# Stream pieces in other slots and load order, routing in column groups with the bias rows behind the first gather, and other ScalarE and VectorE orders around attention

## The chip, the cores and the metric

One core of one Trainium2 chip runs the whole program in one launch. The metric is the device time of an execution in microseconds (us). A core has TensorE (PE, products; PEld is its weight load), VectorE (DVE), ScalarE (ACT), GpSimd (POOL, hardly used here) and SyncE (SP), which in this kernel issues every large DMA. Each engine works off its own queue in order and waits on semaphores.

## The reference

`first_block` and then `second_block` on 256 tokens of 1024 channels, all in fp32. Cut to what matters:

```python
# first block
proj = rmsnorm(x) @ w_mix_in            # short conv, gated delta rule, stick-breaking attention -> y
x = x + y @ w_mix_out
u = causal_dwconv(rmsnorm(x) @ w_ffn_up)
x = x + (silu(gate) * val) @ w_ffn_down
x = rmsnorm(x) * w_norm_final
# second block
sh1, sc1, gt1, sh2, sc2, gt2 = split(silu(c) @ w_ada + b_ada)
h = rms_norm(x, g_pre_mix) * (1 + sc1) + sh1
dq, dk, dv, nq, nk, nv = split(h @ w_in)      # differential and 2-D neighbourhood attention
mix = concat(o_diff, o_nat) @ w_out
x = x + gt1 * rms_norm(mix, g_post_mix)
h2 = rms_norm(x, g_pre_ffn) * (1 + sc2) + sh2
logits = h2 @ w_router + b_router             # 32 experts, top 4, softmax of the four
y[e] = swiglu_clamped(h2[tokens of e] @ w1[e] + b1[e]) @ w2[e] + b2[e]
x = x + gt2 * rms_norm(sum_k gate_k * y[expert_k], g_post_ffn)
```

## The kernel before

**Weights.** All weights ahead of the experts are 46 pieces of 2 MB (128 x 4096 fp32), and the parts are called `inp` (first projection, 7 pieces), `ada` (modulation, 12), `mo` (mix-out, 2), `up` (11), `dn` (down, 6), `in2` (second block's projection, 6) and `out` (2). The table `N_OF` gives each piece a number n. Piece n lies in slot n % 4 of a ring, and SP's `load(n)` (L317) first waits for `used(n - 4)`: the products that read the piece that lies there. The order in which SP loads is written out by hand (L322 to L376) and need not be that of the numbers. The experts' weights are 192 pieces of 2 MB in 10 slots (the four of the ring, four more, and slots 8 and 9 in the work area); a pass of the expert stage takes one expert's tokens in groups of 32 (53 passes here), and one expert has 6 pieces.

**Products.** Dense fp32 products are made of three: a weight piece is split into `w_hi` (ScalarE's copy, L1344, on VectorE for a few) and `w_lo` (VectorE, L1350), and the same is done to the activations (`x_hi`, `x_lo`). `rows_hi` and `rows_lo` (L1355, L1361) do it for mix-out and out. Two `w_hi` buffers take turns. `ada(j)` (L805) is a product of few rows. On TensorE `in2_hi(j, ..)` and `in2_lo(j, ..)` are the parts of projection piece j (L945, L946); its last part signals `proj2`, which both frees the slot and lets ScalarE copy the result (`projected(g)`, L1588, two for each piece).

**Attention.** TensorE weaves the projection and attention together in a fixed order: `score_pair(u)` (L988), `turn(v)` (transposes of probabilities, L1001), `diff_apply(v)` (L1013), `nat_apply`. Two waits of that order matter: `proj2_in` at 4 ahead of `score_pair(0)` and at 6 ahead of `diff_apply(0)`. ScalarE's order there:

```python
w_hi(a, i_in2 + 3)
projected(2)
projected(3)
probs(0)
probs(1)
w_hi(a, i_in2 + 4)
probs(2)
projected(4)
probs(3)
projected(5)
evac(0)
```

**Routing.** After `out`'s products and a norm come the logits (L1125), transposes of the activations (L1130), a mask of the top four on VectorE, positions of the tokens (L1135 to L1141), the sorting of the experts by load on VectorE, the table of passes (`cum`), the place of each token by pass (PP) and its gate (GP) (L1166 to L1170), the bias rows of b2 that open the four output banks (L1178), and then the first gather (L1185) with its transpose (L1192) and the first pass (L1210).

Of the kernel before, what the change touches and what calls it, by code (L numbers as in the profile page):

```python
# [26 lines left out]
P = 128  # L27
# [47 lines left out]
def first_block_and_moe(nc, consts, vecs, stream, bada, rows, natb, w1, w2, b1, b2, x, out):  # L75
    ctx = ExitStack()
    with ctx:
# [9 lines left out]
        def S(name):  # L87
            if name not in sems:
# [9 lines left out]
            pe_step=("ab ab_sum gcol gb kk krow xi_t vrow qsum at uw b0 a12 qq13 qq2 s2 o0 s3 o modc0 modc1 modc2 lams yd_turned lg pos posrow pmt cum pp"),  # L98
            act_step=("ab_in e_gates gl decays ksilu silc dt krow_in vsilu xi_in sk_root qsilu q_squares vrow_in "
                      "uw_in s1 s2_in s3_in o_squares o_root elam d_root yd_hi ee"),  # L100
            dve_step=("wab gu a8 egl dt_arg scales xit qs atm qe a1 qq13_in a2 qq2_in o_var sc_prod "
                      "lamp nlam d_var d_scaled yd_lo mask lgs cnr perm cum_in"))
# [25 lines left out]
        def three(ap, a):  # L128
            return ap.rearrange("p (a b) -> p a b", a=a)
# [100 lines left out]
        OUT_HI = (HI[0], LO[0])  # L230
# [11 lines left out]
        B1 = at(EX, 2048)  # L242
# [8 lines left out]
        LG, MASK, EE, GATE, PM = (three(temp(64), T) for _ in range(5))  # L251
# [15 lines left out]
        H2R = XN  # L267
        slot_base = [len([n for n in range(NSTREAM) if n % NSLOT1 == s]) if s < NSLOT1 else 0 for s in range(NSLOT)]
# [43 lines left out]
        def _(sp):  # L312
# [22 lines left out]
            for piece_ in (("dn", 0), ("dn", 1), ("dn", 2), ("dn", 3), ("in2", 0), ("dn", 4), ("dn", 5), ("ada", 8), ("ada", 9), ("ada", 10)):  # L335
                load(N_OF[piece_])
# [4 lines left out]
            for piece_ in (("out", 0), ("in2", 3), ("in2", 4), ("in2", 5), ("out", 1)):  # L341
                load(N_OF[piece_])
# [9 lines left out]
            expert_piece(0, 2)  # L352
            expert_piece(1, 7)
            sp.wait_ge(S("sc_in"), 16)
            for part in range(3):
                sp.dma_start(B1[NE * part:NE * part + NE, :], b1).then_inc(S("b1_in"), 16)
# [7 lines left out]
            expert_piece(0, 0)  # L364
# [3 lines left out]
            sp.dma_start(B2[0:NE, :], b2).then_inc(S("b_in"), 16)  # L368
# [181 lines left out]
        def _(pe):  # L550
# [303 lines left out]
            ada(2)  # L854
            pe.wait_ge(S("mo_gdn"), 2)
            mo_rows(0, 0)
            sb_tail(0)
# [68 lines left out]
            ada(9)  # L926
            ada(10)
            pe_norm(3)
            ada(11)
# [109 lines left out]
            in2_hi(0, 0, 4)  # L1039
            in2_lo(0, 0, 4)  # L1040
# [79 lines left out]
            hT_ready(pe, 4)  # L1120

            wr = three(vec("router"), KC)
            for t in range(T):
                for k in range(KC):
                    last = mm(flat[:, 2048 + 32 * t:2048 + 32 * t + 32], HT[:, k, 128 * t:128 * t + 128], wr[:, k, :],  # L1125
                              start=(k == 0), stop=(k == KC - 1))
            last.then_inc(*signal("lg"))
            for t in range(T):
                for k in range(KC):
                    last = nc.tensor.transpose(flat[:, 1024 * t + 128 * k:1024 * t + 128 * k + 128],  # L1130
                                               HT[:, k, 128 * t:128 * t + 128], ident)
                last.then_inc(S("h2r"), 1)
# [1256 lines left out]
```

## Time and profile before

| | |
|---|---|
| median of 3 runs | 1542.11 us (1541.65 to 1543.21) |
| the profiled execution's own time | 1541.02 us |
| its span | 1539.2 us |
| TensorE busy | 1337.1 us (87%) |
| VectorE busy | 542.9 us (35%) |
| ScalarE busy | 440.4 us (29%) |
| chain that ended last | PE 52%, DMA 36%, DVE 7%, ACT 3%, issue 2% |
| DMA | 509.28 MB, 331 GB/s over the span |

The profiled execution is 1.1 us below the median of the runs and 1.8 us above its span. Shares are averages over the program: the rows further down are taken by stage. The first block's mixer runs to about 196 us, up and down to 401, the second block's norm and modulation to 419, projection and attention with the out products to 552, routing to 594, the expert passes to 1526. PEclk in a row of windows is the granted clock of TensorE, as a share of 2.4 GHz (0.50 is 1.2 GHz).

### The profile page before, as it was taken

How to read it: one execution, taken by the hardware profiler on the slowest of the kernel's cores; microseconds unless marked ns; L12 is line 12 of the kernel's file. 1: busy time of each engine (PE TensorE's matmuls, PEld its weight loads, DVE VectorE, ACT ScalarE, POOL GpSimd, SP SyncE). 2: the span in 40 equal slices, each digit the busy share in tenths (PEclk: the TensorE clock that was granted, in tenths of full speed). 3: DMA queues.
4: the chain of work that ended last, by engine and by line, in shares of the span. 5: the costliest groups of instructions: out<-in, count | busy, mean ns of one | idle time of the engine just before them, and what ended most of it. 6: DMA issues, size and time to landing. Idle time of an engine off the chain costs nothing.

```text
span 1539.2 us, 30880 instructions
## 1 busy us (share of the span) xinstructions
PE 1337.1 (87%) x13128; PEld 779.5 (51%) x13128; DVE 542.9 (35%) x1075; ACT 440.4 (29%) x730; POOL 0.2 (0%) x4
## 2 busy tenths in 40 slices
PE   6999889999998868889988898789878798787985
PEld 5998569998688653334333333223323243232331
DVE  5842558784666752112121121112112121111212
ACT  5734334453355531112122111112111122121121
POOL 0000000000000000000000000000000000000000
PEclk9999999999999987899999999889999899999997
DMA  7322684454862476997999999999999999999996
GB/s 325 129 111 108 276 369 171 172 208 167 329 246 88 161 322 260 427 384 289 400 428 427 420 407 427 427 427 402 427 428 428 427 407 428 427 427 407 412 427 280
DMA packets 35988, 509.28 MB, mean 331 GB/s; under 512 B 4032, under 2 KB 4032, under 8 KB 4832
## 3 DMA queue, kind: packets, MB, share of 16 engines
q1 hardware_dynamic: 35904, 508.00, 79.5%
q8 instruction: 73, 1.20, 0.3%
q14 instruction: 11, 0.09, 0.0%
HBM read 506.93 MB, written 1.05 MB: 330 GB/s over the span
## 4 chain that ended last, share of the span: by engine, by line
PE 52%; DMA 36%; DVE 7%; ACT 3%; issue 2%; SPq 0%; DVEq 0%; ACTq 0%
DMA low<-in_w 26%; PE acc L1210 14%; PE acc L469 8%; PE acc L1227 7%; DMA high_part<-in_w 7%; DMA low<-in_stream 3%; PE acc L505 3%; PE acc L908 3%; PE acc L945 2%; PE acc L916 1%; PE acc L506 1%; PE acc L1200 1%; PE acc L832 1%; PE acc L805 1%; ACT w_hi L1344 1%
## 5 line engine op out<-in xcount | busy, mean ns | idle before, releaser
L1210 PE MATMUL acc<-low,high_part 128*32 128x512 f32 x2720 | 342.9, 636 | 74.6 <-DMA low<-in_w 64.6
L2238 DVE TENSOR_SCALAR high_part<-acc 128x256 f32<-128x256 f32 x53 | 22.5, 425 | 689.5 <-PE acc L1210 689.5
L1210 PEld LDWEIGHTS acc<-low,high_part 128*32 128x32 f32 x2720 | 93.0, 114 | 281.4 <-issue 194.8
L1227 PE MATMUL acc<-low,high_part 128*32 128x256 f32 x2752 | 165.4, 389 | 28.3 <-DMA low<-in_w 27.9
L1718 ACT ACTIVATE high_part<-high_part 128x256 f32<-128x256 f32 x53 | 22.1, 418 | 451.7 <-DVE high_part L2238 451.7
L1350 DVE TENSOR_TENSOR w_lo<-low,w_hi 128x4096 fp32r<-128x4096 f32 x30 | 132.6, 4424 | 36.8 <-ACT w_hi L1344 36.7
L1227 PEld LDWEIGHTS acc<-low,high_part 128*32 128x32 f32 x2752 | 84.2, 111 | 94.5 <-DMA low<-in_w 36.5
L1344 ACT ACTIVATE w_hi<-low 128x4096 fp32r<-128x4096 f32 x28 | 101.6, 3629 | 55.7 <-DMA low<-in_stream 33.0
L1210 PE MATMUL acc<-high_part 128*32 128x512 f32 x672 | 86.9, 641 | 18.4 <-DMA high_part<-in_w 16.4
L469 PE MATMUL acc<-x_hi,w_hi 128*128 128x256 f32 x352 | 86.8, 287 | 7.1 <-DVE x_lo L1378 7.1
L469 PE MATMUL acc<-x_lo,w_hi 128*128 128x256 f32 x352 | 86.6, 287 | 0.0
L1727 ACT ACTIVATE high_part<-acc 128x256 f32<-128x256 f32 x53 | 20.4, 386 | 210.2 <-PE acc L1227 210.2
L1200 PE MATMUL acc<-high_part 32*128 32x256 f32 x864 | 78.3, 432 | 0.6 <-ACT high_part L1727 0.5
L469 PEld LDWEIGHTS acc<-x_hi,w_hi 128*128 128x128 f32 x352 | 69.0, 196 | 8.0 <-DVE w_hi L1342 8.0
L469 PEld LDWEIGHTS acc<-x_lo,w_hi 128*128 128x128 f32 x352 | 69.0, 196 | 0.0
L1718 ACT ACT_TABLE_LOAD x53 | 68.0, 1283 | 1.4 <-issue 0.5
L1200 PEld LDWEIGHTS acc<-high_part 32*128 32x128 f32 x864 | 34.3, 186 | 59.4 <-issue 57.9
L1185 PE MATMUL acc<-high_part 128*32 128x256 f32 x864 | 59.4, 394 | 0.0
L1210 PEld LDWEIGHTS acc<-high_part 128*32 128x32 f32 x672 | 23.2, 114 | 69.5 <-issue 46.7
L505 PE MATMUL acc<-x_hi,w_hi 128*128 128x256 f32 x176 | 44.2, 290 | 0.0
L469 PE MATMUL acc<-x_hi,w_lo 128*128 128x256 f32 x352 | 44.0, 283 | 0.0
L1966 DVE SCALAR_TENSOR_TENSOR low<-acc,high_part,low 128x255 f32<-128x255 f32 (+1 forms) x88 | 36.4, 476 | 21.4 <-ACT low L1566 21.1
(454 smaller groups left out, 1766.2 us busy)
## 6 DMA issues: line engine op xcount, KB each, us to landing
low<-in_w SPq DMA_DIRECT2D x154, 2048.0 KB, 27.8
low<-in_stream SPq DMA_DIRECT2D x46, 2048.0 KB, 7.9
high_part<-in_w SPq DMA_DIRECT2D x38, 2048.0 KB, 29.8
high_part<-in_natb SPq DMA_DIRECT2D x1, 2048.0 KB, 17.6
high_part<-in_rows SPq DMA_DIRECT2D x1, 1536.0 KB, 18.4
high_part<-in_consts SPq DMA_DIRECT2D x1, 1060.0 KB, 6.9
high_part<-in_x SPq DMA_DIRECT2D x1, 1024.0 KB, 4.8
out<-high_part SPq DMA_DIRECT2D x2, 512.0 KB, 2.7
```

The costliest lines, as they stand in the source:

```text
L469: return nc.tensor.matmul(o, w[:, k, cols], x[:, k, :], **flags)
L505: return nc.tensor.matmul(o, w[:, k, cols], x[:, k, :], skip_group_check=True, **flags)
L908: last = mm(bank(2 * t + h), g[:, k, 128 * t:128 * t + 128], wh[:, o:o + 512], start=(k == 0 and g is gh), stop=False)
L945: return mm(o, w[:, k, cols], x[:, k, :], skip_group_check=True, **flags)
L1185: last = mm(flat[32 * q:32 * q + 32, 3072:3328], SEL[:, t, :], H2R[:, t, 256 * q:256 * q + 256], start=(t == 0), stop=(t == T - 1))
L1200: last = mm(flat[:, o:o + 256], SGT[r, 128 * t:128 * t + 128], YS[r, :], start=False, stop=False, skip_group_check=True)
L1210: last = mm(flat[32 * q:32 * q + 32, 2048:2560], XG[:, b, 32 * kk:32 * kk + 32], wp[:, 2048 * b + 512 * q:2048 * b + 512 * q + 512], start ...
L1227: last = mm(flat[32 * q:32 * q + 32, 3072:3328], AT[:, 128 * (c % 2) + 32 * (c // 2):128 * (c % 2) + 32 * (c // 2) + 32], wp[:, 1024 * (c ...
L1344: eng.activation(HI[i % 2], slot, ACT.Copy).then_inc(S("hi_act"), 1)
L1350: v.tensor_tensor(LO[s], ring[:, s, :], HI[i % 2].bitcast(F32), ALU.subtract).then_inc(S("lo_ready"), 1)
L1718: f(SIG, GLU, ACT.Sigmoid, scale=1.702).then_inc(S("sig"), 1)
L1966: last = stt(uc[:, 256 * c + sh:256 * c + 256], flat[:, o + 256 * c:o + 256 * c + 256 - sh], fc3[:, j, 3 * c + tap:3 * c + tap + 1], uc[:, ...
```

## The change

It renumbers the stream pieces (which slot each lies in and so which products its load waits for), reorders SP's loads, and reorders and reshapes work around them. The core of the diff:

```diff
-for _part, _ns in (("inp", range(PIN)), ("ada", (7, 9, 11, 13, 15, 12, 17, 19, 37, 34, 36, 41)), ("mo", (8, 10)),
-                   ("up", (14, 16, 21, 23, 18, 20, 25, 27, 22, 24, 29)), ("dn", (31, 26, 28, 33, 30, 32)),
-                   ("in2", (35, 40, 38, 39, 44, 42)), ("out", (45, 43))):
+for _part, _ns in (("inp", range(PIN)), ("ada", (7, 9, 11, 13, 15, 17, 19, 14, 37, 34, 32, 41)), ("mo", (8, 10)),
+                   ("up", (12, 21, 23, 18, 16, 25, 27, 22, 20, 29, 31)), ("dn", (26, 24, 33, 35, 30, 28)),
+                   ("in2", (39, 36, 38, 40, 42, 44)), ("out", (45, 43))):
...
-        OUT_HI = (HI[0], LO[0])
+        OUT_HI = (HI[0], LO[2])
...
-        B1 = at(EX, 2048)
+        B1 = W(6, 2048)
...
-            for piece_ in (("inp", 5), ("inp", 6), ("ada", 0), ("mo", 0), ("ada", 1), ("mo", 1), ("ada", 2), ("ada", 3), ("ada", 4),
-                           ("ada", 5), ("ada", 6), ("ada", 7)):
+            for piece_ in (("inp", 5), ("inp", 6), ("ada", 0), ("mo", 0), ("ada", 1), ("ada", 2), ("mo", 1), ("ada", 3), ("ada", 4),
+                           ("up", 0), ("ada", 5), ("ada", 6), ("ada", 7)):
                 load(N_OF[piece_])
-            sp.wait_ge(S("sb_y"), 2)
+            sp.dma_start(MODR[1], bada[:, 512:1024]).then_inc(S("bada_in"), 16)
             sp.dma_start(at(BC, 3072), rows).then_inc(S("rows_in"), 16)
-            load(N_OF["up", 0])
-            sp.dma_start(MODR[1], bada[:, 512:1024]).then_inc(S("bada_in"), 16)
...
-            for piece_ in (("out", 0), ("in2", 3), ("in2", 4), ("in2", 5), ("out", 1)):
+            for piece_ in (("out", 0), ("out", 1), ("in2", 3), ("in2", 4), ("in2", 5)):
                 load(N_OF[piece_])
...
-            sp.dma_start(B2[0:NE, :], b2).then_inc(S("b_in"), 16)
+            for q in range(4):
+                sp.dma_start(B2[NE * q:NE * q + NE, :], b2).then_inc(S("b_in"), 16)
...
-            ada(2)
             pe.wait_ge(S("mo_gdn"), 2)
             mo_rows(0, 0)
+            ada(2)
...
+            pe_norm(3)
             ada(10)
-            pe_norm(3)
-            ada(11)
...
             in2_hi(0, 0, 4)
+            ada(11)
             in2_lo(0, 0, 4)
...
-            hT_ready(pe, 4)
             wr = three(vec("router"), KC)
+            for b in range(4):
+                pe.wait_ge(S("hT_act" if b % 2 else "hT_dve"), 2 * 1 + b // 2 + 1)
+                for k in (2 * b, 2 * b + 1):
+                    q = k % 4
+                    last = mm(flat[32 * q:32 * q + 32, 2048:2304], wr[:, k, :], HT[:, k, :], start=(k < 4), stop=(k >= 4))
+            last.then_inc(*signal("lgp"))
...
             for t in range(T):
-                for k in range(KC):
-                    last = mm(flat[:, 2048 + 32 * t:2048 + 32 * t + 32], HT[:, k, 128 * t:128 * t + 128], wr[:, k, :],
-                              start=(k == 0), stop=(k == KC - 1))
+                last = mm(flat[:, 2560 + 32 * t:2560 + 32 * t + 32], LP[:, 128 * t:128 * t + 128], STACK, start=True, stop=True)
             last.then_inc(*signal("lg"))
...
-            pe.wait_ge(S("h2r_in"), 2)
-            pe.wait_ge(S("b_in"), 16)
-            pe.wait_ge(S("b1_parts"), B1PARTS)
-            for t in range(T):
-                for h in range(2):
-                    mm(bank(2 * t + h), GTT[0:32, 128 * t:128 * t + 128], B2[0:32, 512 * h:512 * h + 512],
-                       start=True, stop=False, skip_group_check=True)
...
             gather_transpose()
+            pe.wait_ge(S("b_in"), 64)
+            for q in range(4):
+                t, h = divmod(q, 2)
+                r = slice(32 * q, 32 * q + 32)
+                mm(bank(q), GTT[r, 128 * t:128 * t + 128], B2[r, 512 * h:512 * h + 512], start=True, stop=False, skip_group_check=True)\
+                  .then_inc(S("b2_in"), 1)
+            pe.wait_ge(S("b1_parts"), B1PARTS)
...
             evac(1)
+            w_hi(a, i_in2 + 5)
+            projected(6)
             probs(6)
             probs(7)
+            projected(7)
+            evac(2)
             diff_o(1)
-            w_hi(a, i_in2 + 5)
-            projected(6)
-            projected(7)
-
-            evac(2)
...
+            a.wait_ge(*step("pmt"))
+            f(PMT[0:32], flat[0:32, 3584:3840], ACT.Copy)
+            f(GTT, flat[:, 3840:4096], ACT.Copy).then_inc(*signal("pmt_in"))
...
-            rows_lo(N_OF["out", 0], OUT_HI[0], "out_w_hi0", 1, "out_w_lo0")
             softmax(8)
...
             weigh(11)
+            rows_lo(N_OF["out", 0], OUT_HI[0], "out_w_hi0", 1, "out_w_lo0")
             v.wait_ge(*step("yd_hi"))
...
-            v.wait_ge(*step("pmt"))
-            link(v.tensor_copy(PMT[0:32], flat[0:32, 3584:3840]))
-            v.tensor_copy(GTT[0:32], flat[0:32, 3840:4096]).then_inc(S("pmt_in"), 1)
```

Not shown: the residual after mix-out now has VectorE's `w_hi` of up(0) ahead of it; the split of b1 (VectorE) moves from behind attention to ahead of it and b1 is loaded behind down's pieces; `rows_lo` of out(1) moves behind `nat_lo(1)`; the gates are transposed four times over, so that each row group has its copy; the activations' transposes are split into three groups around the logits and positions; ScalarE copies H2R[0]; `select(0)` stands right behind the copy of PP; expert 0's piece 0 is loaded first among its pieces and piece 2 last but one, in place of the other way round.

Three places show how the work moves. The first is SP's queue around the end of the first block's mixer; L320 (L321 after) is `load`, and the words in brackets are the semaphores that it waits for. Before:

```order
L320 DMA low<-in_stream 128x4096 [waits proj] x6
L320 DMA low<-in_stream 128x4096 [waits ada] x3
L320 DMA low<-in_stream 128x4096 [waits mo_k]
L320 DMA low<-in_stream 128x4096 [waits ada] x2
L330 DMA high_part<-in_rows 128x3072 [waits sb_y]
L320 DMA low<-in_stream 128x4096 [waits mo_done]
L332 DMA low<-in_bada 128x512
```

After:

```order
L321 DMA low<-in_stream 128x4096 [waits proj] x5
L321 DMA low<-in_stream 128x4096 [waits ada]
L321 DMA low<-in_stream 128x4096 [waits proj]
L321 DMA low<-in_stream 128x4096 [waits ada] x2
L321 DMA low<-in_stream 128x4096 [waits mo_k]
L321 DMA low<-in_stream 128x4096 [waits ada] x2
L321 DMA low<-in_stream 128x4096 [waits mo_done]
L330 DMA low<-in_bada 128x512
L331 DMA high_part<-in_rows 128x3072
```

The load that waits for mo_k is ada(5) before and up(0) after; the one that waits for mo_done is up(0) before and ada(7) after. The transfer of `rows` has lost its wait and stands behind them.

The second place is ScalarE's queue at the start of attention; w_hi_50 and w_hi_49 are the two buffers of L1344 (L1355 after). Before:

```order
L1344 ACTIVATE w_hi_50<-low 128x4096 [waits lo_ready,hi_used,slot3_loaded]
L1588 ACTIVATE low<-acc 128x512 [waits proj2] x2
L1594 ACTIVATE low,high_part<-low,high_part 128x256 [waits nmax]
L1594 ACTIVATE low,high_part<-low,high_part 128x256
L1594 ACTIVATE low,high_part<-low,high_part 128x256 [waits nmax]
L1594 ACTIVATE low,high_part<-low,high_part 128x256
L1344 ACTIVATE w_hi_49<-low 128x4096 [waits lo_ready,hi_used,slot0_loaded]
L1594 ACTIVATE low,high_part<-low,high_part 128x256 [waits nmax]
L1594 ACTIVATE low,high_part<-low,high_part 128x256
L1588 ACTIVATE low<-acc 128x512 [waits proj2]
```

After:

```order
L1355 ACTIVATE w_hi_50<-low 128x4096 [waits lo_ready,hi_used,slot0_loaded]
L1599 ACTIVATE low<-acc 128x512 [waits proj2] x2
L1605 ACTIVATE low,high_part<-low,high_part 128x256 [waits nmax]
L1605 ACTIVATE low,high_part<-low,high_part 128x256
L1605 ACTIVATE low,high_part<-low,high_part 128x256 [waits nmax]
L1605 ACTIVATE low,high_part<-low,high_part 128x256
L1355 ACTIVATE w_hi_49<-low 128x4096 [waits lo_ready,hi_used,slot2_loaded]
L1605 ACTIVATE low,high_part<-low,high_part 128x256 [waits nmax]
L1605 ACTIVATE low,high_part<-low,high_part 128x256
L1599 ACTIVATE low<-acc 128x512 [waits proj2]
```

The order is the same and the slots are others: in2(3) waits for slot 0, where in2(1) lies ahead of it, in place of slot 3 with in2(0); in2(4) for slot 2 behind in2(2), in place of slot 0 behind in2(1).

The third place is TensorE's queue from GP's products to the first pass. Before:

```order
L1170 MATMUL acc<-high_part 128x64 x2
L1178 MATMUL acc<-high_part 128x512 [waits b1_parts,b_in,h2r_in]
L1178 MATMUL acc<-high_part 128x512 x3
L1185 MATMUL acc<-high_part 32x256 [waits dve_step,sel]
L1185 MATMUL acc<-high_part 32x256 x7
L1192 MATMUL acc<-high_part 128x128 [waits pmt_in,g_in]
L1192 MATMUL acc<-high_part 128x128
```

After:

```order
L1181 MATMUL acc<-high_part 128x64 x2
L1188 MATMUL acc<-high_part 32x256 [waits h2r_in,sel]
L1188 MATMUL acc<-high_part 32x256 x7
L1195 MATMUL acc<-high_part 128x128 [waits g_in]
L1195 MATMUL acc<-high_part 128x128
L1272 MATMUL acc<-high_part 128x512 [waits b_in]
L1272 MATMUL acc<-high_part 128x512 x3
```

The four bias rows (L1178 before, L1272 after) stand behind the gather (L1185, L1188) and its transpose (L1192, L1195). The trace counts each such fp32 matmul as two.

## Rows read from the trace of the kernel before

**Rows 1.** Windows by stage: span, busy by engine (instructions), granted clock, DMA share, GB/s

```profile
420.00:552.00 132.00, 120.16 (x762) 101.63 (x761) 87.10 (x123) 69.34 (x141) 0.00 (x0) 0.96 0.50 197
552.00:594.00 42.00, 27.32 (x134) 19.75 (x132) 19.91 (x75) 8.64 (x18) 0.00 (x0) 0.64 0.61 243
594.00:1526.00 932.00, 799.24 (x8983) 315.13 (x8986) 166.66 (x528) 165.65 (x317) 0.00 (x0) 0.94 0.97 410
```

**Rows 2.** Page, costliest groups: busy, mean ns | idle before, releaser

```profile
L1210 PE MATMUL acc<-low,high_part 128*32 128x512 f32 x2720 | 342.9, 636 | 74.6 <-DMA low<-in_w 64.6
```

**Rows 3.** Chain that ended last, 145 to 212 us: start, duration, what

```profile
149.67 10.76 DMA low<-in_stream
...
196.40 11.70 DMA low<-in_stream
```

**Rows 4.** The same chain, 440 to 500 us

```profile
479.58 3.50 ACT w_hi L1344
...
484.60 2.08 PE acc L1013 x8
```

**Rows 5.** Timeline of TensorE, first up product: start, us [idle before <-releaser]

```profile
211.35 0.55 PE L469 MATMUL acc<-x_hi,w_hi 128*128 128x256 f32 x1 [7.11 <-DVE x_lo L1378]
```

**Rows 6.** Page, DMA issues: KB each, us from issue to landing

```profile
low<-in_stream SPq DMA_DIRECT2D x46, 2048.0 KB, 7.9
```

**Rows 7.** Timeline of TensorE at the second block's norm

```profile
414.95 1.92 PE L805 MATMUL acc<-low,high_part 128*32 128x512 f32 x16
...
418.69 0.39 PE L945 MATMUL acc<-x_hi,w_hi 128*128 128x256 f32 x1 [1.16 <-DVE x_lo L1401]
```

**Rows 8.** Short windows, columns as in Rows 1

```profile
209.00:215.00 6.00, 3.65 (x17) 3.68 (x18) 6.00 (x11) 1.33 (x1) 0.00 (x0) 0.50 1.00 425
484.00:488.00 4.00, 3.40 (x16) 3.40 (x17) 3.61 (x1) 1.45 (x7) 0.00 (x0) 0.50 0.03 6
```

**Rows 9.** Timeline of SP's issues

```profile
444.75 0.33 SPq L320 DMA_DIRECT2D low<-in_stream  x1
...
458.23 0.33 SPq L320 DMA_DIRECT2D low<-in_stream  x1
```

**Rows 10.** Timeline of ScalarE at the start of attention

```profile
444.50 1.07 ACT L1588 ACTIVATE low<-acc 128x512 f32<-128x512 f32 x2
...
453.38 3.63 ACT L1344 ACTIVATE w_hi<-low 128x4096 fp32r<-128x4096 f32 x1
...
459.36 0.57 ACT L1588 ACTIVATE low<-acc 128x512 f32<-128x512 f32 x1
```

**Rows 11.** Timeline of TensorE: score_pair(0) and diff_apply(0)

```profile
448.31 1.13 PE L988 MATMUL acc<-low 64*128 64x256 f32 x8
...
463.51 1.06 PE L1013 MATMUL acc<-low,high_part 128*128 128x128 f32 x8
```

**Rows 12.** Page, the group of VectorE's weight splits

```profile
L1350 DVE TENSOR_TENSOR w_lo<-low,w_hi 128x4096 fp32r<-128x4096 f32 x30 | 132.6, 4424 | 36.8 <-ACT w_hi L1344 36.7
```

**Rows 13.** Chain that ended last, 552 to 612 us

```profile
565.01 5.01 PE acc L1125 x32
570.02 3.47 PE acc L1130 x16
...
579.79 0.42 DVE high_part L2206
...
583.08 6.93 PE acc L1178 x8
590.01 1.91 PE acc L1185 x16
```

**Rows 14.** Timeline of VectorE: last step towards the mask

```profile
572.01 0.22 DVE L2167 TENSOR_TENSOR high_part<-high_part 128x64 f32<-128x64 f32 x1
```

**Rows 15.** Timeline of TensorE: products of 32 rows in a pass

```profile
603.34 0.71 PE L1200 MATMUL acc<-high_part 32*128 32x256 f32 x8
```

**Rows 16.** Timeline of TensorE: the first pass

```profile
594.39 1.94 PE L1210 MATMUL acc<-low,high_part 128*32 128x512 f32 x8 [1.28 <-ACT high_part L1713]
```

More of the change, by code:

```diff
@@ L249, in temp @@
             return at(tmp[0] - n, n)
-        LG, MASK, EE, GATE, PM = (three(temp(64), T) for _ in range(5))
+        LG, MASK, EE, PM = (three(temp(64), T) for _ in range(4))
         LX, MR = three(temp(80), T), three(temp(80), T)
@@ L1123, in _ @@
+            pe.wait_ge(*step("lgp_in"))
+            pe.wait_ge(*step("stack"))
             for t in range(T):
-                for k in range(KC):
-                    last = mm(flat[:, 2048 + 32 * t:2048 + 32 * t + 32], HT[:, k, 128 * t:128 * t + 128], wr[:, k, :],
-                              start=(k == 0), stop=(k == KC - 1))
+                last = mm(flat[:, 2560 + 32 * t:2560 + 32 * t + 32], LP[:, 128 * t:128 * t + 128], STACK, start=True, stop=True)
             last.then_inc(*signal("lg"))
-            for t in range(T):
[L1129 to L1132, printed above, removed]
@@ L1134, in _ @@
-            pe.wait_ge(*step("mask"))
-            mm(flat[:, 2560:2592], before, MASK[:, 0, :], start=True, stop=True)
-            mm(flat[:, 2592:2624], before, MASK[:, 1, :], start=True, stop=False)
-            mm(flat[:, 2592:2624], ones, MASK[:, 0, :], start=False, stop=True)
+            for k in range(4, KC):
+                last = nc.tensor.transpose(flat[:, 128 * k:128 * k + 128], HT[:, k, 0:128], ident)
+            last.then_inc(S("h2r"), 1)
+            pe.wait_ge(*step("mask"))
@@ L1140, in _ @@
-            for t in range(T):
-                last = mm(flat[0:32, 2625:2625 + NE], ones[:, 0:32], MASK[:, t, :], start=(t == 0), stop=(t == T - 1))
+                last = mm(flat[0:32, 3137:3137 + NE], ones[:, 0:32], MASK[:, t, :], start=(t == 0), stop=(t == T - 1))
             last.then_inc(*signal("pos"))
+            for k in range(KC):
+                last = nc.tensor.transpose(flat[:, 1024 + 128 * k:1024 + 128 * k + 128], HT[:, k, 128:256], ident)
+            last.then_inc(S("h2r"), 1)
@@ L1147, in _ @@
               .then_inc(*signal("posrow"))
             pe.wait_ge(S("gate"), 2)
-            for i, a in enumerate((PM, GATE)):
-                for t in range(T):
-                    o = 3584 + 256 * i + 128 * t
-                    last = nc.tensor.transpose(flat[0:32, o:o + 128], a[:, t, :], ident)
+            for t in range(T):
+                o = 3584 + 128 * t
+                nc.tensor.transpose(flat[0:32, o:o + 128], PM[:, t, :], ident)
+                last = mm(flat[:, o + 256:o + 384], GATE4[:, t, :], ident, start=True, stop=True)
@@ L1162, in _ @@
+            mm(flat[0:1, 2656:2688], CNR[0:32], PERM[0:32], start=True, stop=True)
+            mm(flat[0:1, 2688:2720], const("rank")[0:32, NE + 1:NE + 2], PERM[0:32], start=True, stop=True)
+            mm(flat[0:1, 2720:2721], CNR[0:32], ones[0:32, 0:1], start=True, stop=True).then_inc(*signal("cum"))
+            pe.wait_ge(*step("pmt_in"))
             pe.wait_ge(S("oh"), 2)
@@ L1993, in _ @@
             split_hT(link, 3)
-            modulation(2)
             lam = vec("lam")
@@ L2113, in _ @@
             weigh(13)
-            rows_lo(N_OF["out", 1], OUT_HI[1], "out_w_hi1", 1, "out_w_lo1")
             softmax(14)
@@ L2227, in select @@
                 last.then_inc(S("sel"), 1)
+            v.wait_ge(*step("cum"))
+            v.tensor_copy(passes[0:1, 0:32], flat[0:1, 2624:2656])
+            v.tensor_copy(passes[0:1, 32:64], flat[0:1, 2656:2688])
+            link(v.tensor_copy(LAST[0:1], flat[0:1, 2624:2656]))
+            stt(passes[0:1, 72 + NE:72 + 2 * NE], LAST[0:1], -1.0, flat[0:1, 2656:2688], ALU.add, ALU.add)
+            v.tensor_copy(passes[0:1, 72:72 + NE], flat[0:1, 2688:2720])
+            v.tensor_copy(passes[0:1, 64:65], flat[0:1, 2720:2721]).then_inc(*signal("cum_in"))
+            v.wait_ge(*step("pp"))
+            link(v.tensor_copy(PP, three(flat[:, 2048:2048 + T * NPMAX], T)))
+            select(0)
+            for part in (1, 2):
+                link(v.tensor_copy(OH[NE * part:NE * part + NE, :], OH[0:NE, :]))
+            v.wait_ge(*step("gp"))
+            link(v.tensor_copy(GP, three(flat[:, 3584:3584 + T * NPMAX], T)))
+            v.memset(SGT, 0.0).then_inc(S("sgt_in"), 1)
+            v.memset(YS, 0.0).then_inc(S("y_in"), 1)
             def select_gated(p):
```

120 lines of the change are left out of this document (59 added, 61 removed).

## The prediction, made before the changed kernel was run

> **What bounds the kernel now.** I read the table by stage first [rows 1]. From 594 to 1526 us the DMA engines are busy 0.97 of the time at 410 GB/s, and the page charges TensorE's idle time in its costliest group there to weights that have not landed [rows 2]: 74.6 us before L1210, 64.6 of them behind low<-in_w. This expert stage reads a fixed 192 pieces and is bound by DMA, so it costs the same whatever is done ahead of it; what counts is when it can begin. Ahead of it the roles are reversed: in 420 to 552 us DMA has half a load (0.50) and TensorE works 120.16 of 132 us, with 11.8 us idle in all; in 552 to 594 us, the routing, TensorE waits on short hops between engines, and the granted clock averages 0.64. The change touches only what lies ahead of 594 us. So every microsecond by which the first pass (594.39) moves should appear whole in the end. The chain of waits gives the places where time is lost: two loads that are issued late, landing at 160.4 and 208.1 [rows 3], and in attention a ScalarE split for which the next product has to wait [rows 4].
>
> **Early loads: -13.3 us.** Before, ada(2) stands on TensorE's queue ahead of mo_rows(0, 0) and its load, issued at 149.67, takes 10.76 us [rows 3]. The load is now ahead of mo(1)'s, and the product behind mo_rows, which has its data. By hand bookkeeping of slot releases the mix-out products end at about 190.3 instead of 196.4. There the second loss begins: up(0) is issued at 196.40 and takes 11.70 us to land [rows 3], so that the up products start only at 211.35 [rows 5]. Now up(0) lies in slot 0, free with mo(0)'s products, and is resident by about 183; what is loaded behind mo(1) is ada(7): 190.3 and 7.9 us [rows 6] is 198.2, and its product 1.9 us (as L805 at 414.95 [rows 7]), so that up starts at 200.2, 11.15 earlier. The half clock of 209 to 215 us [rows 8] follows TensorE's 7.11 us without work [rows 5]; with the short gap that is left I take it away: 3.65 us busy at 0.50 is worth 1.8, with the piece behind 215 some 2.1 us. Together -13.3 us; bounds -9 (ada(7) lands 2 us later behind the rows' transfer, half clock stays) and -15.
>
> **Block 2's norm and ada(11): +2.1.** The norm's transposes need not wait for ada(10) now, but behind them the same VectorE chain runs to the first projection product (before at 418.69 [rows 7], four matmuls ahead of it); I carry 418.2 over as 405.1, 13.1 earlier. ada(11), 1.92 us, moves from ahead of in2_hi(0), where it hid behind VectorE, into the dense products: it is paid. in2(1)'s products, over before when SP issued the load behind them at 444.75 [rows 9], end at about 433.5.
>
> **Attention: from -11.2 to +19.9.** A load waits for the piece four numbers ahead. Before, in2(3), (4), (5) wait for in2(0), (1), (2); now for in2(1), (2), (3), each a whole piece later. The order of work on ScalarE is the same: w_hi, then projected, then what TensorE waits for. Before, SP issued in2(4) at 444.75 and in2(5) at 458.23 [rows 9], so that neither held anything up for long.
> - First: in2(3) issued 433.5, landed 7.9 later, w_hi 3.63, two projections 1.07 [rows 10]: score_pair(0) at 446.1, before 448.31 [rows 11]. The lead of 11.2 is down to 2.2. TensorE has idled 8 us by then, so I add 1.7 of half clock (3.40 us busy at 0.50 in 484 to 488 [rows 8], after the like stop); in2(2) then ends at 457.7 (9.9 us of work, 448.31 to 458.2).
> - Second: in2(4) issued 457.7, landed 465.6, w_hi until 469.2. Behind it on ScalarE stand probs(2), projected(4), probs(3), projected(5), 2.9 us (from 453.38 + 3.63 to 459.36 + 0.57 before [rows 10]), and diff_apply(0) waits for the last: about 473, before 463.51 [rows 11]. +9.5. VectorE's w_lo of in2(3), 4.42 us [rows 12], stands behind weigh(3), which waits for probs(3); by the bookkeeping it ends near 482, and in2(3)'s low products and its release, with score_pair(6) and diff_apply(1) between, come at about 488.4.
> - Third: in2(5) issued 488.4, landed 496.3, w_hi until 499.9. Behind it now also stand projected(6), probs(6), probs(7), projected(7) and evac(2), 4.5 us in all: diff_apply(2) at 504.5, before 484.60 [rows 4]. +19.9.
> - The rest: there is no further load to wait for (out(0) and out(1) lie there long before). rows_lo of out(0), just ahead of yd_lo now, exposes up to 4.4 us [rows 12]; waits of TensorE on VectorE give back up to 5. I take 0, range -5 to +4. The out products end 19.9 later.
>
> **The Trainium skill on the load.** "DMA: Bandwidth & Descriptors", section "Anatomy of one DMA", gives 2.0 us and the bytes at 436 GB/s for a DMA of the other issue path. By that, an estimate from the page, 2 MB would land in 6.8 us; the trace has 7.9, so the measurement decides. By the page's figure three loads would cost 3.3 us less and the sum would be 5.8.
>
> **Routing: -10.8 us**, read from [rows 13] where no other group is named.
> - Logits: 5.01 us of 128x32 matmuls. Now 8 matmuls in four column groups (like the gather's 8, 1.91 us), of which only the last two, 0.5, follow the last quarter of the norm; then ScalarE's copy of 128x256 (about 0.4, as VectorE's of 256), two small products (four records of 5.01/32, 0.6), two hops: 1.8. -3.2.
> - The 3.47 us of transposes ended at 573.49, VectorE's last step towards the mask at 572.2 [rows 14]; most go behind: -1.0.
> - The copies of PMT and GTT leave VectorE's chain (0.42 each) for ScalarE, which is idle there: -0.9.
> - The bias rows, 6.93 us ahead of the gather at 590.01, move behind gather_transpose; the gather waits for the copy of PP and the select, 0.8 us, during which the 0.85 us of GP's products, ahead of 583.08 now, run. -7.0.
> - There they are four matmuls in four row groups. Nearest row: eight 32-row records of 256 columns took 0.71 us at full clock [rows 15]; 512 columns double it, half clock doubles it again: 2.6 us, of which ScalarE's copy and the wait before the pass hide 1.3 (the 1.28 that TensorE waited there [rows 16]). +1.3. Bounds: 0, and +5.6 if they run one after another as now.
> The skill's "TensorE: Matmul & The Clock Gate", "Measured speedup vs the span model", has 3.07 for four row tiles of K=32, N=512. By that figure 6.93 would become 2.3; the row gives 2.6, and the sum would be 0.3 lower.
>
> **Sum.** -13.3 + 2.1 and then in place of -11.2 the +19.9 of the third stall (so attention alone costs 31.1), -10.8 in routing: +9.1. The profiled execution's 1541.0 becomes 1550.1; against the median of 1542.1, 1551.2. DMA work that grows (b1 and the four copies of b2, small) lies in stages with half a load.
>
> **Rivals.**
> - *Stalls are partly paid back* (0.10). While TensorE stands still, VectorE and ScalarE finish softmaxes, so that its 11.8 us of waits in 420 to 552 [rows 1] vanish. For: VectorE is only 87 of 132 us busy. Against: the ScalarE queue is in order and its exponentials stand behind the late split. All of it: -2.7, 1539.4.
> - *Only the first load bites* (0.07), the case on the other side. If what stands between release and use is longer than 11.5 us for in2(4) and in2(5), attention ends with the lead of 2.2 that the first one leaves: -2.2 - 10.8 = -13.0, 1529. It decides when in2(4) is issued before about 447; against it, it needs in2(2)'s products to be over by then.
> - *The slots make no difference* (0.03): all loads early enough. -11.2 - 10.8 = -22, 1520.
> - *The early gain is lost* (0.10): ada(7)'s load, with bada, rows and up(1) near it, or the split of up(0) ahead of the residual, delays the norm by about half of the gain. +9.1 + 6.6: 1557.8.
>
> **How the numbers follow.** My forecast, three late loads against two gains, has 0.70, with a range of its own of 1544 to 1557 (-5 and +4 of the rest, the clock, the bias rows). A change under 0.2% (3.1 us) can't be told from none here. Faster by more: 0.10 (two rivals); within it 0.08 (payback); slower 0.82. The range for 8 in 10 is 1541.5 to 1558.5.
>
> **What would show it.** In the profile after: up's first product near 200, at full clock; TensorE idle about 8 us before score_pair(0), then before diff_apply(0) and diff_apply(2), ScalarE's w_hi waiting for slots 0, 2, 0 with DMA named; the end of the out products near 572 and the first pass about 31 us behind it instead of 42; the expert stage of unchanged length (932 us). I am wrong if the three w_hi find their pieces landed, if TensorE's idle time moves out of attention, or if the expert stage gets longer: then a different wait rules.

## The result and the profile after

The changed kernel takes 1552.88 us (median of 4 runs, 1552.66 to 1554.21), the kernel before beside it 1541.88 us (1540.06 to 1543.21). The ratio is 1.0082 with a 95% interval of 1.007 to 1.0093: slower by some 12.6 us by the ratio, 11.0 by the medians. The forecast was 1551.2 us. The profiled execution took 1552.79 us with a span of 1551.0, 11.8 us longer than the one before by both figures.

The windows by stage of the changed kernel, columns as in [rows 1] (span, busy by engine, granted clock, DMA share, GB/s), for attention from the end of in2(1), routing, and 932 us of expert stage from the first pass:

```profile
437.00:575.00 138.00, 101.99 (x570) 83.78 (x569) 67.92 (x111) 59.22 (x134) 0.00 (x0) 0.85 0.34 130
575.00:606.50 31.50, 21.08 (x127) 14.70 (x130) 18.61 (x73) 11.55 (x22) 0.00 (x0) 0.60 0.77 296
606.50:1538.50 932.00, 799.05 (x8998) 315.75 (x9001) 166.70 (x528) 164.41 (x317) 0.00 (x0) 0.95 0.97 411
```

The page's group of the expert stage that answers to [rows 2]:

```profile
L1213 PE MATMUL acc<-low,high_part 128*32 128x512 f32 x2720 | 341.6, 634 | 73.4 <-DMA low<-in_w 64.5
```

The expert stage is what it was, the same 932 us with DMA busy 0.97; its first pass moved by 12.05 us, from 594.39 [rows 16] to 606.44, and the end by 11.8. Routing, from the last out product to the first pass, has shrunk from 42.15 us to 31.3. Attention has grown, with TensorE idle 36 of 138 us and a granted clock of 0.85 in place of 0.96.

The chain of waits of the changed kernel around the start of the up products (start, duration, what), which answers to [rows 3] and [rows 5]:

```profile
190.74 9.94 DMA low<-in_stream
...
200.72 3.64 PE acc L808 x16
204.37 5.69 PE acc L472 x39
```

ada(7)'s load is issued when the mix-out products end, at 190.74 (190.3 was forecast), but takes 9.94 us, and its product runs at half clock. TensorE has nothing else to do for the last 4.00 us of it (timeline; the bracket is the idle time before, and what ended it):

```profile
200.72 3.64 PE L808 MATMUL acc<-low,high_part 128*32 128x512 f32 x16 [4.00 <-DMA low<-in_stream]
```

Two short windows of the changed kernel show the half clock in the first up products and just behind score_pair(0):

```profile
201.00:206.00 5.00, 5.00 (x24) 2.10 (x17) 1.50 (x2) 0.00 (x0) 0.00 (x0) 0.50 1.03 438
449.00:453.00 4.00, 3.35 (x11) 2.42 (x12) 1.16 (x2) 0.50 (x2) 0.00 (x0) 0.50 0.00 0
```

In attention the chain shows the same step three times, a load released late and then ScalarE's split of it:

```profile
437.25 7.64 DMA low<-in_stream
...
444.92 3.62 ACT w_hi L1355
...
462.26 7.83 DMA low<-in_stream
...
470.11 3.62 ACT w_hi L1355
...
492.18 7.80 DMA low<-in_stream
```

And TensorE's timeline shows what waits for them, score_pair(0), diff_apply(0) and diff_apply(2), with the idle time ahead of each in brackets (compare [rows 11] and [rows 4]):

```profile
449.65 1.65 PE L990 MATMUL acc<-low 64*128 64x256 f32 x6 [8.78 <-ACT low L1599]
...
477.27 1.62 PE L1015 MATMUL acc<-low,high_part 128*128 128x128 f32 x6 [9.57 <-ACT high_part L1615]
...
507.96 1.41 PE L1015 MATMUL acc<-low,high_part 128*128 128x128 f32 x5 [11.54 <-ACT high_part L1623]
```

29.9 us of idle time stand ahead of these three. Routing's part of the chain, which answers to [rows 13]:

```profile
586.67 2.04 PE acc L1128 x16
588.71 0.59 PE acc L1131 x4
...
598.16 0.27 ACT high_part L1726
...
601.30 1.93 PE acc L1188 x16
...
604.42 2.02 PE acc L1272 x8
606.44 1.87 PE acc L1213 x8
```

The logits now come in 2.04 us. While ScalarE copies them TensorE makes some of the transposes (L1131), and two small products follow. The gather starts at 601.30 right behind GP's products, and the four bias rows take 2.02 us between it and the first pass.

| step | forecast | changed kernel's trace |
|---|---|---|
| mix-out products end | 190.3 | 190.7 |
| up starts | 200.2 | 204.4 |
| in2(1)'s products end | 433.5 | 437.2 |
| score_pair(0) | 446.1 | 449.65 |
| diff_apply(0) | 473 | 477.3 |
| in2(3)'s products end | 488.4 | 492.2 |
| diff_apply(2) | 504.5 | 508.0 |
| out products end, against before | +19.9 | +22.9 |
| routing | -10.8 | -10.8 |
| all | +9.1 | +11.8 |

### The profile page after: what moved, and what is told of

The parts are those of the page before. It is cut to its first block, busy times and chain, and to the rows that moved or that the text cites. A ratio compares the mean times of both kernels' runs of the same rounds, so it can differ in the third digit from the quotient of the medians.

```text
span 1551.0 us, 30918 instructions
## 1 busy us (share of the span) xinstructions
PE 1336.3 (86%) x13118; PEld 778.9 (50%) x13118; DVE 541.8 (35%) x1073; ACT 441.8 (28%) x734; POOL 0.2 (0%) x4
## 4 chain that ended last, share of the span: by engine, by line
PE 54%; DMA 36%; DVE 6%; ACT 2%; issue 2%; SPq 0%; DVEq 0%; ACTq 0%
DMA low<-in_w 28%; PE acc L1213 14%; PE acc L472 8%; PE acc L1230 8%; DMA high_part<-in_w 4%; DMA low<-in_stream 4%; PE acc L508 3%; PE acc L911 3%; PE acc L947 3%; PE acc L919 1%; PE acc L509 1%; PE acc L1203 1%; PE acc L443 1%; PE acc L808 1%; PE acc L948 1%
## 5 line engine op out<-in xcount | busy, mean ns | idle before, releaser
L1355 ACT ACTIVATE w_hi<-low 128x4096 fp32r<-128x4096 f32 x28 | 101.6, 3629 | 101.4 <-DMA low<-in_stream 76.0
L1188 PE MATMUL acc<-high_part 128*32 128x256 f32 x864 | 59.3, 393 | 0.0
L1230 PE MATMUL acc<-high_part 128*32 128x256 f32 x640 | 38.7, 389 | 5.4 <-DMA high_part<-in_w 5.4
## 6 DMA issues: line engine op xcount, KB each, us to landing
high_part<-in_w SPq DMA_DIRECT2D x38, 2048.0 KB, 29.9
high_part<-in_rows SPq DMA_DIRECT2D x1, 1536.0 KB, 13.4
```

Source lines behind the costliest of these rows:

```text
L1188: last = mm(flat[32 * q:32 * q + 32, 3072:3328], SEL[:, t, :], H2R[:, t, 256 * q:256 * q + 256], start=(t == 0), stop=(t == T - 1))
L1230: last = mm(flat[32 * q:32 * q + 32, 3072:3328], AT[:, 128 * (c % 2) + 32 * (c // 2):128 * (c % 2) + 32 * (c // 2) + 32], wp[:, 1024 * (c ...
L1355: eng.activation(HI[i % 2], slot, ACT.Copy).then_inc(S("hi_act"), 1)
```

## The experiments

Each ratio below is to the kernel before on the same chip, with its 95% interval; a time in us is that ratio's difference from 1 times 1541.9. Where I compare positions in two traces I count from the end of the down products to the start of the last nat_apply, because the start of up varies by itself (last section). That end is 400.7 in the kernel before and 392.65 in the changed one.

### No load late, the first late, two late

The first edit puts in2(3), (4), (5) behind in2(0), (1), (2) again. The rest of the change stays:

```diff
-                   ("in2", (39, 36, 38, 40, 42, 44)), ("out", (45, 43))):
+                   ("in2", (39, 36, 38, 43, 40, 42)), ("out", (45, 44))):
...
-        OUT_HI = (HI[0], LO[2])
+        OUT_HI = (HI[0], LO[3])
...
-            for piece_ in (("out", 0), ("out", 1), ("in2", 3), ("in2", 4), ("in2", 5)):
+            for piece_ in (("out", 0), ("in2", 3), ("in2", 4), ("in2", 5), ("out", 1)):
```

Expert 0's pieces 2 and 0 change places in SP's order, as their slots come free at other times.

> The changed kernel, with in2(3), (4), (5) behind in2(0), (1), (2) again (in2 in pieces 39, 36, 38, 43, 40, 42, out in 45, 44, and the slots of out(1)'s split and of expert 0's last pieces to match). Theory: three late loads cost what the changed kernel's trace shows between the end of in2(1)'s products (7.5 us ahead of the kernel before) and diff_apply(2) (23.4 behind), 30.9 us, and all of it ends up in the time: 1552.9 - 30.9 = 1522. Rival, payback: TensorE's waits for VectorE in attention, 11.8 us in the kernel before, are already hidden in the stalls of the changed kernel and come back without them, so only about 19 us are gained: 1534.

In the second, in2(3) alone is late (in2(4) has the piece behind in2(0), the rest as in the first):

```diff
-                   ("in2", (39, 36, 38, 40, 42, 44)), ("out", (45, 43))):
+                   ("in2", (39, 36, 38, 40, 43, 42)), ("out", (45, 44))):
...
-            for piece_ in (("out", 0), ("out", 1), ("in2", 3), ("in2", 4), ("in2", 5)):
+            for piece_ in (("out", 0), ("in2", 4), ("in2", 3), ("in2", 5), ("out", 1)):
```

> As the run with no late load, but in2(3) waits for in2(1) (pieces 39, 36, 38, 40, 43, 42): only the first of the three loads is late. Theory: 11.5 us over that run (7.5 ahead becomes 4.0 behind by the end of in2(2)'s products in the changed kernel's trace), so 1533.5. Rival: VectorE's softmaxes bound the stretch behind it, TensorE waited there anyway, and the first stall costs 4 us or less: 1526.

In the third, in2(3) and in2(4) are late, and in2(5) has the early piece. OUT_HI stays as in the changed kernel, and expert 0's last pieces are reordered once more:

```diff
-                   ("in2", (39, 36, 38, 40, 42, 44)), ("out", (45, 43))):
+                   ("in2", (39, 36, 38, 40, 42, 43)), ("out", (45, 44))):
...
-            for piece_ in (("out", 0), ("out", 1), ("in2", 3), ("in2", 4), ("in2", 5)):
+            for piece_ in (("out", 0), ("in2", 5), ("in2", 3), ("in2", 4), ("out", 1)):
```

> As the changed kernel, but in2(5) has piece 43 and waits for in2(0): the first two loads are late, the third is not. Theory: the third stall takes diff_apply(2) from 16.9 behind to 23.4 behind, 6.5 us, so 1546.4. Rival: each late load costs the same third of 30.9, so 1542.6; or the third is hidden behind VectorE, so that nothing changes: 1553.

Measured: none late 0.9833 (0.9816 to 0.9849), -25.7 us; the first late 0.9905 (0.9888 to 0.9921), -14.6; two late 0.9985 (0.9975 to 0.9994), -2.3; all three, the changed kernel, 1.0082. So the three loads are worth 11.1, 12.3 and 15.0 us, 38.4 together. The traces, from the end of down to the start of the last nat_apply, have 136.3, 147.2, 158.7 and 172.1 us: 10.9, 11.5 and 13.4, 35.8 together. ScalarE's splits of in2(3), (4), (5) in the run with none late (timeline; the bracket is its idle time before):

```profile
433.39 3.63 ACT L1355 ACTIVATE w_hi<-low 128x4096 fp32r<-128x4096 f32 x1 [6.05 <-DMA low<-in_stream]
...
443.64 3.63 ACT L1355 ACTIVATE w_hi<-low 128x4096 fp32r<-128x4096 f32 x1
...
460.93 3.63 ACT L1355 ACTIVATE w_hi<-low 128x4096 fp32r<-128x4096 f32 x1 [0.26 <-issue]
```

and in the run with two late:

```profile
443.75 3.62 ACT L1355 ACTIVATE w_hi<-low 128x4096 fp32r<-128x4096 f32 x1 [15.61 <-DMA low<-in_stream]
...
468.54 3.62 ACT L1355 ACTIVATE w_hi<-low 128x4096 fp32r<-128x4096 f32 x1 [14.05 <-DMA low<-in_stream]
...
485.79 3.63 ACT L1355 ACTIVATE w_hi<-low 128x4096 fp32r<-128x4096 f32 x1 [0.25 <-issue]
```

Without the late slots ScalarE never waits for a DMA again from the second split on; with two late the third is taken up with no wait for a load. The rival of payback is out: the run with none late is better than the theory by 6 us, not worse by 12, and TensorE's one long wait for VectorE in this stage, ahead of the out products, is the same with and without the stalls (4.83 us and 4.82). The first two steps are as expected (11.5 and 12.9). The third is not: it was to be worth 6.5 and is worth 15.0 (13.4 in the traces), and together the three cost 38.4 (35.8 in the traces), not 30.9. The largest part of both misses has one cause: I measured the third stall against the kernel before, whose diff_apply(2) itself waited 4.89 us for ScalarE (the chain of [rows 4] runs through ScalarE to this product). That is the whole of 35.8 less 30.9. In the run with none late that wait is nearly gone:

```profile
470.97 1.13 PE L1015 MATMUL acc<-low,high_part 128*128 128x128 f32 x8 [0.99 <-ACT high_part L1623]
```

### ScalarE's order at in2(5)

With none late, what still differs on ScalarE in attention between this run and the kernel before is that the change has w_hi(in2(5)) and projected(6) ahead of probs(6) and probs(7). The edit, made to the run with none late and to the changed kernel:

```diff
             evac(1)
-            w_hi(a, i_in2 + 5)
-            projected(6)
             probs(6)
             probs(7)
-            projected(7)
-            evac(2)
             diff_o(1)
+            w_hi(a, i_in2 + 5)
+            projected(6)
+            projected(7)
+            evac(2)
```

> The run with no late load (ratio 0.9833), with ScalarE's order of the kernel before: w_hi(in2(5)) behind probs(6), probs(7), diff_o(1). Theory: that order, not the slots, had held up diff_apply(2) in the kernel before by its 4.9 us wait for ScalarE, and the new order takes that away where no load is late: +4.9 over the run with no late load, ratio 0.9865. Rival: the run with no late load is ahead of the sum of my parts for another reason (in2(5)'s slot or the place of b1), and the order changes nothing: 0.9833.

> The changed kernel with ScalarE's old order at the same place. Theory: with in2(5)'s load late, probs(6) and probs(7) can run while it is under way instead of behind its split, so the old order is better here: diff_apply(2) follows the split by projected(6), projected(7) and evac(2) alone, -2.6, ratio 1.0065. Rival: the new order is better here too, +2 to +5: 1.010 or more.

Measured: with none late and the old order 0.9878 (0.9863 to 0.9893) against 0.9833, 6.9 us worse; in the changed kernel with the old order 1.0048 (1.0036 to 1.0061) against 1.0082, 5.2 us better. By the traces, from the end of down to the start of the last nat_apply, it is +5.0 (141.3 against 136.3) and -3.2 (168.9 against 172.1). The theories were +4.9 and -2.6; by the times the second is missed by more than the interval of its ratio (1.0065 expected). TensorE's timeline at diff_apply(2) with none late and the old order:

```profile
478.22 2.08 PE L1015 MATMUL acc<-low,high_part 128*128 128x128 f32 x8 [4.90 <-ACT high_part L1615]
```

and in the changed kernel with the old order:

```profile
504.64 1.65 PE L1015 MATMUL acc<-low,high_part 128*128 128x128 f32 x6 [8.69 <-ACT high_part L1615]
```

The 4.89 us of the kernel before are back in the first, as 4.90. In the second the idle time is 8.69 instead of 11.54: there ScalarE had its exponentials done by 495.1, while the load was under way, and the split followed at 499.52, when the load had landed. In the changed kernel ScalarE stood still for the 12.90 us ahead of that split and ran them behind it. So the new order is by the traces a gain of 5 us where the load is in time and a loss of 3 where it is late (7 and 5 by the times), and the changed kernel has the loss.

### Routing alone, all but routing

The diff falls into two halves that run by themselves: the routing part (the logits, transposes, copies and bias rows; the matching lines on TensorE, ScalarE, VectorE and the four loads of b2) on the kernel before, and everything else on it.

> The kernel before with the routing part of the change alone (column groups for the logits, transposes split up, copies on ScalarE, bias rows in row groups behind the gather). Theory: the first pass comes 10.8 us earlier and all of it counts: 1541.9 - 10.8 = 1531.1. Rival: expert 0's last pieces or slots 8 and 9 are not landed that early when attention is not stalled, and half of it is lost: 1536.5.

> The kernel before with all of the change except its routing part. Theory: the parts add, so the out products end 22.9 us later than before and the old routing follows: 1541.9 + 22.9 = 1564.8. Rival: part of the routing's gain in the changed kernel came from the loads of expert weights having more time behind a stalled attention, so that without the new routing less is lost: under 1560.

Measured: routing alone 0.9922 (0.9906 to 0.9939), -12.0 us; all but routing 1.0145 (1.0116 to 1.0174), +22.4, where the theories had -10.8 and +22.9. The sum, +10.3, is the changed kernel's +12.6 within the intervals. The chain of the run with routing alone, from the last out product to the first pass:

```profile
549.99 1.83 PE acc L453 x8
...
577.13 1.94 PE acc L1187 x16
...
580.26 2.02 PE acc L1271 x8
582.28 1.73 PE acc L1212 x8
```

From 551.82 to 582.28 are 30.5 us, where the kernel before has 42.15 and the changed one 31.3. The rival that the weights of expert 0 would not be there is out: the pass starts behind the bias rows, and from the first pass to the end of the span this run has 944.3 us, the kernel before 944.8, the changed one 944.6, the one with all but routing 943.0. The expert stage shifts whole, with first passes from 582 to 619 us. The rival of the other run, that less would be lost than 18 us without the new routing, is out too. The parts of routing ahead of the bias rows (logits, transposes, copies) were not run one by one, and neither were the early loads and the place of ada(11): what I say of those rests on the traces alone.

### The bias rows: the place or the row groups

In both runs the four products go back ahead of the first gather of the changed kernel. In one they are all in the first group of 32 rows (the diff); in the other `r` stays `slice(32 * q, 32 * q + 32)`:

```diff
+            pe.wait_ge(S("h2r_in"), 2)
+            pe.wait_ge(S("b_in"), 64)
+            for q in range(4):
+                t, h = divmod(q, 2)
+                r = slice(0, 32)
+                mm(bank(q), GTT[r, 128 * t:128 * t + 128], B2[r, 512 * h:512 * h + 512], start=True, stop=False, skip_group_check=True)\
+                  .then_inc(S("b2_in"), 1)
             pe.wait_ge(S("sel"), 1)
             pe.wait_ge(S("h2r_in"), 2)
...
-            pe.wait_ge(S("b_in"), 64)
-            for q in range(4):
-                t, h = divmod(q, 2)
-                r = slice(32 * q, 32 * q + 32)
-                mm(bank(q), GTT[r, 128 * t:128 * t + 128], B2[r, 512 * h:512 * h + 512], start=True, stop=False, skip_group_check=True)\
-                  .then_inc(S("b2_in"), 1)
```

> The changed kernel with the four bias rows ahead of the first gather again and all in the first row group, as in the kernel before. Theory: 6.9 us come back onto the path and the 1.3 us that ScalarE's copy did not cover behind the gather go: +5.7, 1558.6. Rival: the gather's operands are not ready then anyway (the copy of PP, the select), which hides about 1 us: 1557.5.

> The changed kernel with the bias rows ahead of the first gather, but in four row groups as it has them. Theory: the row groups carry most of the gain and the place little: the 2.0 us stand ahead of the gather, less the 0.7 to 1.3 that they cost behind it: +0.7 to +1.3, 1554. Rival: the place is what matters, because the products of 32 rows share nothing at half clock: +5, 1558.

Measured: one group 1.0114 (1.0083 to 1.0145), four groups 1.0074 (1.0046 to 1.0102). The intervals are wider than what is sought and hold the changed kernel's 1.0082 in the second case, so the traces have to tell. The chain with one group:

```profile
599.80 6.93 PE acc L1268 x8
606.73 1.91 PE acc L1188 x16
...
611.18 1.93 PE acc L1213 x8
```

and with four:

```profile
601.61 2.03 PE acc L1268 x6
603.64 1.91 PE acc L1188 x16
...
608.09 1.94 PE acc L1213 x8
```

From the end of the out products to the first pass it is 37.6 us with one group and 32.4 with four, ahead of the gather both times, and 31.3 in the changed kernel. The row groups carry 5.1 us and the place 1.1, so the rival that the place is what matters is out; 6.93 us became 2.03 by the groups alone. What the place is worth with one group was not run.

### ada(7) behind up(0)

```diff
             pe_norm(2)
-            ada(7)
...
                 if j == 1:
+                    ada(7)
                     pe.wait_ge(S("modr"), 2)
...
+            w_lo(i_up)
             modulation(1)
-            w_lo(i_up)
```

and SP's transfer of `rows` goes behind down's loads.

> The changed kernel, but ada(7)'s product stands behind up(0)'s on TensorE, VectorE's w_lo of up(0) ahead of modulation(1), and the transfer of rows behind down's loads. Theory: in the changed kernel up waits 4.0 us for ada(7)'s load and 3.6 for its product at half clock although up(0) is resident and x_lo ready from 197; without it up starts near 197 at full clock and up(1) follows ada(7)'s product: about -5.5, 1547.4. Rival: up(1)'s load and ScalarE's split of it (ready at 213.6 in the changed kernel) then set the pace, and moving rows away does not bring it early enough: -2 or less.

Measured: 1.0052 (1.0035 to 1.007), 4.6 us better than the changed kernel, where the theory had 5.5 and the rival 2 or less. The chain of this run:

```profile
195.78 3.23 DVE x_lo L1389 x8
...
199.06 10.33 PE acc L472 x84
209.39 1.90 PE acc L808 x16
```

The up products start at 196.80 behind x_lo, ada(7) has its 1.90 us at full clock behind up(0), and down ends at 388.1 instead of 392.65, 4.5 earlier. In the nine profiled runs with the changed kernel's code up to there down ends between 389.4 and 393.1, in the three with this edit between 388.1 and 388.8. The load took 9.45 us, little less than in the changed kernel; TensorE only has other work meanwhile. The three edits of this run were not tried apart.

### Together

The run with no late load and this edit together, and then also rows_lo of out(0) back to its place ahead of softmax(8):

> The run with no late load together with ada(7) behind up(0). Theory: the two gains lie in different stages and add: 0.9833 less 0.0030 (4.6 us), 0.9803. Rival: in2's or down's loads cannot follow the earlier stage and take half of it back: 0.9818.

> As the run before it, with rows_lo of out(0) ahead of softmax(8) on VectorE, its place in the kernel before. Theory: in the changed kernel's chain these 4.33 us lie bare just ahead of the out products; ahead of softmax(8) they hold up score_pair's consumers by as much, of which TensorE's in2(5) products hide most: -1 to -4 against the run before it. Rival: softmax(8) to (11) are themselves the chain there, and it costs as much as it gains: 0 to +1.

Measured: 0.9804 (0.9791 to 0.9818), -30.2 us, and 0.9808 (0.9793 to 0.9824). The first is the best version of all, some 1512 us; the two gains add. The second is the same within the interval: TensorE reached the first nat_apply at 510.5 and at 510.6, although the 4.33 us of rows_lo stood bare on the chain of the changed kernel. Its rival was right: TensorE's wait of 4.82 us ahead of the out products is gone, and waits of 2.85 us for VectorE, at score_pair, and of 1.38 and 0.48 behind it have come in its place.

## Why the prediction was right

The time and its sign came out as forecast, and by the mechanism forecast: three late loads against two gains ahead of and behind them. The sum is closer than its parts. Early loads missed by 5.2 us, and 2.2 of these came back where I had counted nothing or too much.

- **What bounds.** That a shift of the first pass counts whole was right: from it to the end of the span the runs have 943.0 to 945.4 us, with first passes from 565 to 619 us.
- **Early loads, -13.3.** This term was mis-sized: down ends 8.1 earlier, outside even the bounds of -9 and -15. The mix-out products end as computed. ada(7) then took 9.94 us to land where I put 7.9, its product 3.64 at half clock where I put 1.9, and the half clock of the up products, which I took away, was there again for 2 us. The bound of -9 had the late landing and the half clock of the up products in it, but not the product of ada(7) at half clock. I had treated the wait for ada(7) as too short to matter; TensorE stood still for 4.0 us.
- **Norm and ada(11), +2.1.** It was +0.6, so that in2(1) ends 7.5 ahead of before and not 11.2. From the end of down to in2(0)'s first product are 15.8 us in place of 17.95, where I had counted on the same length. The products from there to the end of in2(1), with ada(11) among them, take 28.8 in place of 26.0.
- **Attention, 31.1 from the end of in2(1) to the out products' end.** The trace has 30.4, and 30.9 up to diff_apply(2). The changed kernel's own steps came as worked out: from in2(3)'s end to diff_apply(2) 15.8 us against 16.1. The first two stalls are shown one by one by the runs. What I had wrong is what the third is made of. I read the new order on ScalarE only as more work behind the split; it has a gain of 5 us where no load is late and a loss of 3 where the load is, and the late load by itself costs 13 to 15. The sum holds all the same, since it compares diff_apply(2) with its place in the kernel before, behind that kernel's own wait of 4.89 us: the two parts that I did not see are both in that one difference.
- **The rest, 0.** -0.5 from diff_apply(2) to the last out product, and this is two terms that cancel: a wait of 4.82 us for VectorE ahead of the out products is new, and four waits of the kernel before in that stretch, 6.0 us in all, are gone.
- **Routing, -10.8.** Right in sum. Two parts were each off by half a microsecond and cancel: the gather starts 11.6 earlier in the stage and not 12.1, and the first pass follows it 0.8 later and not 1.3. The bias rows were put at 2.6 us and took 2.0; the row that this was read from, 0.71 us doubled twice, gives 2.8.
- **Rivals.** Payback and "only the first load bites" are refuted by the runs with none and with one late. That the slots make no difference is refuted by the 38 us between the run with none late and the changed kernel. That the early gain is lost was half true: 5 of 13 us were, and by ada(7)'s load. That bada, rows and up(1) slow it, as this rival had it, is not shown (last section).

The difference between the times and the traces for the parts (38.4 against 35.8 us for the slots, 6.9 against 5.0 and 5.2 against 3.2 for the order) lies within the intervals of the ratios, about 2 to 3 us for a difference of two. For two of the three the profiled runs show where it may come from: down ended at 389.4 in the run with none late, at 392.65 in the changed kernel and at 393.1 in the run with none late and the old order, although the code is the same up to there.

## What to carry to other kernels

In a ring of slots the number of a piece decides which product must be over before its load starts: put the next product's weights behind the oldest piece, and count release + landing + split against the work that stands between, since each late one costs that difference anew. An order on an in-order engine can't be judged by itself: moving a split ahead of the exponentials gained 5 us with the load in time and lost 3 with it late, by the traces. Before costing a stall, subtract what the kernel before already waits at the same instruction, and say so, or two effects will be priced as one.

## What the runs showed of the hardware

- A 2 MB load issued alone in attention landed in 7.6 to 7.8 us; the one of ada(7) took 9.94, and 9.45 with `rows` moved away. Three transfers were issued within 2 us behind it, but the load ahead of it, issued at 178.76, was also under way until 192.79. In the changed kernel the load at 163.13, with another ahead of it until 167.71 and none behind it for 12 us, took 9.46, while the one at 175.38, with nothing ahead and 2 MB issued 0.37 us behind it, took 7.67. So a load with 4.6 us still to go ahead costs time by itself, and one issued behind cost nothing there. With 2 us to go ahead, as for ada(7), the loads at 560.89 and 392.68 took 7.81 and 8.99, so that this explains a part of its 9.94 at most. The rest stays open: what the transfers behind it add was not tried by itself.
- The start of the up products, behind this load, lay between 201.9 and 205.1 us in nine profiled runs whose code is the same up to there. About half of that is the load, which landed between 200.0 and 201.4; the other half is the clock at which ada(7)'s product then ran: 1.92 us at a granted clock of 1.00 in the run with none late, 3.64 at 0.50 in the changed kernel. Three microseconds are as much as some of the effects in question, so that positions are better compared from a mark behind it.
- Eight records of 32-row matmuls with 512 columns took 6.93 us in one row group and 2.02 in four, at a granted clock of 0.50 both times: 3.4 times faster for four groups. The page "TensorE: Matmul & The Clock Gate" of the Trainium skill has 3.07 in "Measured speedup vs the span model"; the measurement is a little better.
- The stalls cost more than their idle time: behind score_pair(0), from 449.65 on, TensorE has half clock until about 455 (0.50 in the window 449 to 455), and from there to the end of in2(2)'s products it took 12.6 us instead of 9.9.
